# Column copies of a mixture-of-experts stage: a short loop of 32 copies with unchecked token numbers, the numbers brought in two transfers, and the first block's copies split over two engines

## What is computed

```
xs = ht[slot_tok].reshape(n_blocks, MOE_BLOCK, D)

def expert_block(args):
    xb, e = args
    return (jax.nn.silu(xb @ w_gate[e]) * (xb @ w_up[e])) @ w_down[e]

ys = lax.map(expert_block, (xs, blk_expert)).reshape(P, D)
ys = ys * slot_gate[:, None].astype(ys.dtype)
out = jax.ops.segment_sum(ys, slot_tok, num_segments=T)
```

## Time and profile before

| what | value |
|---|---|
| median of 3 runs | 1705.32 us (1703.37 to 1705.6) |
| the profiled execution, own time | 1699.97 us |
| its span, first to last instruction | 1698.2 us |
| mean granted TensorE clock | 0.976 of full speed |
| PE busy | 1550.6 us, 91% |
| DVE, POOL, ACT busy | 604.2, 451.5, 364.7 us |
| transfers over the span | 472.66 MB, mean 278 GB/s |
| GB/s in slices from about 720 us to the end | 366 to 428, but for the last (245) |

### The profile page before, as it was taken

The page is one execution under the profiler, slowest core; times in us unless marked ns, Lnnn a source line. Parts: engine busy times, 40 slices in busy tenths (PEclk is TensorE's granted clock), DMA queues, the critical chain, the costliest instruction groups (busy, mean ns, idle before and its releaser), DMA issues.

```text
span 1698.2 us, 25999 instructions
## 1 busy us (share of the span) xinstructions
PE 1550.6 (91%) x7036; PEld 857.2 (50%) x7036; DVE 604.2 (36%) x738; ACT 364.7 (21%) x695; POOL 451.5 (27%) x2197
## 2 busy tenths in 40 slices
PE   7999999999999999898988988888889988889897
PEld 7788777678886666533423323333323433333333
DVE  6655666542235334313303213212213312222224
ACT  6422333532222344211001001001001001001001
POOL 4560055310000000233233333223323333233220
PEclk9999999999999999999999999999999999999999
DMA  8333221542314025499999999999899999999996
GB/s 299 102 98 99 74 75 50 199 106 100 99 62 162 1 99 216 179 403 426 428 426 387 402 415 382 404 417 395 366 414 381 408 421 392 375 428 404 371 423 245
DMA packets 89099, 472.66 MB, mean 278 GB/s; under 512 B 5075, under 2 KB 43133, under 8 KB 62973
## 3 DMA queue, kind: packets, MB, share of 16 engines
q1 hardware_dynamic: 87944, 470.84, 69.1%
q0 software_dynamic: 912, 0.35, 0.4%
q10 hardware_dynamic: 100, 0.03, 0.0%
HBM read 466.99 MB, written 4.21 MB: 277 GB/s over the span
## 4 chain that ended last, share of the span: by engine, by line
PE 63%; DMA 26%; DVE 6%; ACT 2%; issue 2%; SPq 0%; DVEq 0%; POOL 0%; ACTq 0%
DMA weight_ring<-in_expert_w_up_dram 25%; PE ps L2283 19%; PE ps L1986 10%; PE ps L1860 10%; PE ps L2309 5%; PE ps L2242 4%; PE ps L2039 3%; DVE residual L1668 2%; PE ps L1822 1%; PE ps L2373 1%; DMA residual<-in_x_dram 1%; PE ps L2102 1%; ACT weight_ring L903 1%; PE ps L1915 1%; PE ps L2099 1%
## 5 line engine op out<-in xcount | busy, mean ns | idle before, releaser
L2283 PE MATMUL ps<-weight_ring,proj_buffer 128*64 128x512 f32 x2024 | 493.1, 619 | 69.3 <-DMA weight_ring<-in_expert_w_up_dram 63.6
L713 POOL COPY proj_buffer<-transposed_acts 128x16 f32 x1982 | 301.9, 212 | 559.8 <-issue 396.7
L2283 PEld LDWEIGHTS ps<-weight_ring,proj_buffer 128*64 128x64 f32 x2024 | 159.5, 142 | 388.7 <-issue 291.9
L1668 DVE TENSOR_TENSOR residual<-ps,residual 128x1024 f32<-128x1024 f32 x128 | 150.9, 1220 | 289.0 <-PE ps L2242 288.5
L2309 PE MATMUL ps<-weight_ring,proj_buffer 128*64 128x512 f32 x960 | 221.0, 614 | 19.5 <-DVE proj_buffer L1678 18.5
L1684 DVE SCALAR_TENSOR_TENSOR y_low<-ps,proj_buffer,y_high 64x1024 fp32r<-64x1024 f32 x60 | 77.0, 1283 | 243.6 <-ACT y_high L1096 242.7
L2309 PEld LDWEIGHTS ps<-weight_ring,proj_buffer 128*64 128x64 f32 x960 | 74.6, 141 | 148.4 <-issue 145.4
L1096 ACT ACTIVATE y_high<-ps,proj_buffer 64x1024 fp32r<-64x1024 f32 x60 | 66.6, 1109 | 296.7 <-PE ps L2309 295.9
L1085 ACT ACTIVATE proj_buffer<-ps 128x512 f32<-128x512 f32 x32 | 19.1, 598 | 485.7 <-PE ps L2283 485.7
L1860 PE MATMUL ps<-mix_high,w_in_high 128*128 128x512 f32 x288 | 117.3, 407 | 1.3 <-issue 1.3
L1860 PE MATMUL ps<-mix_high,w_in_low 128*128 128x512 f32 x288 | 112.3, 390 | 0.0
(11 more groups left out here) (326 smaller groups left out, 1830.4 us busy)
## 6 DMA issues: line engine op xcount, KB each, us to landing
weight_ring<-in_expert_w_down_dram SPq DMA_DIRECT2D x63, 2048.0 KB, 18.4
weight_ring<-in_expert_w_up_dram SPq DMA_DIRECT2D x61, 2048.0 KB, 22.9
weight_ring<-in_expert_w_gate_dram SPq DMA_DIRECT2D x61, 2048.0 KB, 17.8
weight_ring<-in_w_in_dram SPq DMA_DIRECT2D x18, 1024.0 KB, 5.5
weight_ring<-in_w_out_dram SPq DMA_DIRECT2D x16, 1024.0 KB, 5.0
weight_ring<-in_xkv_w_dram SPq DMA_DIRECT2D x8, 1024.0 KB, 7.4
residual<-in_x_dram SPq DMA_DIRECT2D x8, 1024.0 KB, 12.5
weight_ring<-in_expert_w_gate_dram SPq DMA_DIRECT2D x5, 1024.0 KB, 11.8
```

The source lines that it names most:

```text
L713: ins = g.tensor_copy(xsT[:, :, par * SLOTS + at + j], H[:, :, ds(where[j], 1)].rearrange("p k n -> p (k n)"))
L1668: v.tensor_tensor(part, ps[:, bank:bank + 2, :].rearrange("p b n -> p (b n)"), part, ALU.add).then_inc(signal, 1)
L2283: ins = mm(ps[side * SLOTS:(side + 1) * SLOTS, 0, :], xsT[:, k, par * SLOTS:(par + 1) * SLOTS], gate_up_weights(e, u, kk), start=(k == 0), ...
```

## The change

Six edits go together:

- **The short loop.** `copy_columns` makes one stretch of at most 32 columns. For blocks 2 to 31, POOL runs a loop over the blocks with a loop of two stretches inside. `block_rows` counts halves of a block, and PE waits for `b * 2 - 2`.
- **No checks.** The two checking instructions for each value are gone, on ACT too; the numbers are clamped where they are formed, before and after the change.
- **Token numbers.** They lie in DRAM as one row for each block. Blocks 2 to 5 come in one transfer of 1 KB, then all 32 blocks in one of 8 KB into a region of SBUF that is free once block 1's first unit is used. 16 transfers were made before, each issued inside the loop.
- **Block 0** is copied by ACT (36 columns, in two stretches of 18) and POOL (28). DVE's load, checks and 12 copies are gone. PE waits for two signals.
- **Block 1** is split in halves, 32 by ACT and 32 by POOL, and POOL does its half ahead of storing the token numbers to DRAM, which it did after block 0 before.
- The path for further blocks, which isn't taken here, is rewritten in the same way.

```diff
-BY_ACT, BY_DVE = 26, 12
+BY_ACT = 36
@@
-            def copy_columns(tokens, par, first, done, free=None, loaded=None):
-
-                for at in range(first, SLOTS, 32):
-                    n = min(32, SLOTS - at)
-                    _, where = nc.values_load_multi_w_load_instructions(
-                        tokens[:, at:at + n], engines=(mybir.EngineType.Pool,), min_val=0, max_val=S - 1)
-                    if at == 0 and free is not None:
-                        pool.wait_ge(gu_copied, free)
-                    if at + n == SLOTS and loaded is not None:
-                        loaded()
-                    for j in range(n):
-                        ins = g.tensor_copy(xsT[:, :, par * SLOTS + at + j], H[:, :, ds(where[j], 1)].rearrange("p k n -> p (k n)"))
-                ins.then_inc(done, 1)
+            def copy_columns(tokens, slots, before=None):
+
+                n = tokens.shape[1]
+                _, where = nc.values_load_multi_w_load_instructions(
+                    tokens, engines=(mybir.EngineType.Pool,), min_val=0, max_val=S - 1,
+                    skip_runtime_bounds_check_because=CLAMPED)
+                if before is not None:
+                    pool.wait_ge(gu_copied, before)
+                for j in range(n):
+                    ins = g.tensor_copy(slots[:, :, j], H[:, :, ds(where[j], 1)].rearrange("p k n -> p (k n)"))
+                return ins
@@
-            copy_columns(first_row[0:1, 0:SLOTS], 0, BY_ACT + BY_DVE, first_rows[0])
+            copy_columns(first_row[0:1, BY_ACT:SLOTS], xsT[:, :, BY_ACT:SLOTS]).then_inc(first_rows[0], 1)
+            copy_columns(first_row[0:1, SLOTS + 32:2 * SLOTS], xsT[:, :, SLOTS + 32:2 * SLOTS]).then_inc(first_rows[1], 1)
             pool.wait_ge(ids_ready, 1)
@@
-            load_ids(1)
-            with pool.Fori(1, NE // 2) as it:
-                pair_columns(it)
+            def block_columns(b, tokens, at):
+                before = pool.to_reg(b - 1)
+                first = pool.snap(b % 2 * SLOTS)
+                with pool.Fori(0, 2) as half:
+                    copy_columns(tokens[0:1, ds(at + half * 32, 32)],
+                                 xsT[:, :, ds(first + half * 32, 32)], before).then_inc(block_rows, 1)
+
+            load_ids(some_ids, 2, 4)
+            pool.wait_ge(block_ids_in, 16)
+            with pool.Fori(2, 6) as b:
+                block_columns(b, some_ids, b * SLOTS - 2 * SLOTS)
+            pool.wait_ge(used, UE + 7)
+            load_ids(all_ids, 0, NE)
+            pool.wait_ge(block_ids_in, 32)
+            with pool.Fori(6, NE) as b:
+                block_columns(b, all_ids, b * SLOTS)
@@
-            for par, n in enumerate((BY_ACT, 28)):
+            for par, first, last in ((0, 0, 18), (0, 18, BY_ACT), (1, 0, 32)):
@@
-            dve.wait_ge(h_turned, 56)
-            _, where = nc.values_load_multi_w_load_instructions(
-                first_row[0:1, BY_ACT:BY_ACT + BY_DVE], engines=(mybir.EngineType.DVE,), min_val=0, max_val=S - 1)
-            for j in range(BY_DVE):
-                ins = v.tensor_copy(xsT[:, :, BY_ACT + j], H[:, :, ds(where[j], 1)].rearrange("p k n -> p (k n)"))
-            ins.then_inc(first_rows[0], 1)
-
@@
-                    pe.wait_ge(first_rows[b], 3 - b)
+                    pe.wait_ge(first_rows[b], 2)
                 else:
-                    pe.wait_ge(block_rows, b - 1)
+                    pe.wait_ge(block_rows, b * 2 - 2)
```

More of the change, by code:

```diff
@@ L59 @@
 CUT = 3
-BY_ACT, BY_DVE = 26, 12
+BY_ACT = 36
+CLAMPED = "token numbers are sums of one-hot products over tokens, clamped to the last token where they are formed"
 def hybrid_block(nc, x, mem, mix_norm_g, w_in, q_norm_g, k_norm_g, sink_logits, pool_w, pool_scale,
@@ L66, in hybrid_block @@
                  expert_w_gate, expert_w_up, expert_w_down, out):
-    ids_dram = nc.dram_tensor("block_ids", (NBLK // 2 + 1, 2 * SLOTS), I32, kind="Internal").ap()
+    ids_dram = nc.dram_tensor("block_ids", (NBLK, SLOTS), I32, kind="Internal").ap()
     with ExitStack() as ctx:
@@ L161, in hybrid_block @@
         first_row = PB[0:1, 8768:8768 + 2 * SLOTS].bitcast(I32)
+        some_ids = PB[0:1, 8704:8704 + 4 * SLOTS].bitcast(I32)
+        all_ids = PB[0:1, 2048:2048 + NE * SLOTS].bitcast(I32)
         ids = PB[0:NBLK, 9112:9112 + SLOTS].bitcast(I32)
@@ L340, in hybrid_block @@
         ids_stored = sem("ids_stored")
-        pair_ids_in = sem("pair_ids_in")
+        block_ids_in = sem("block_ids_in")
         gu_copied = sem("gu_copied")
@@ L726, in _, with load_ids @@
             pool.wait_ge(ids_stored, 16)
[L728 to L736, removed]
-            load_ids(1)
-            with pool.Fori(1, NE // 2) as it:
-                pair_columns(it)
+            def load_ids(to, first, blocks):
+                pool.dma_start(to, ids_dram[ds(first, blocks), :].rearrange("b s -> (b s)").unsqueeze(0)).then_inc(block_ids_in, 16)
+            def block_columns(b, tokens, at):
[13 more added lines that the diff above has]
+                block_columns(b, all_ids, b * SLOTS)
             more = pool.value_load(meta[0:1, NOVER:NOVER + 1], min_val=0, max_val=NOVER)
             with pool.If(more > 0):
-                with pool.Fori(NE // 2, NBLK // 2) as it:
-                    pair_columns(it)
+                for first in range(NE, NBLK, 4):
+                    load_ids(some_ids, first, 4)
+                    pool.wait_ge(block_ids_in, 16 * (3 + (first - NE) // 4))
+                    with pool.Fori(first, first + 4) as b:
+                        block_columns(b, some_ids, b * SLOTS - first * SLOTS)
         @block.scalar
@@ L1105, in _ @@
             act.wait_ge(hT_ready, 56)
-            for par, n in enumerate((BY_ACT, 28)):
+            for par, first, last in ((0, 0, 18), (0, 18, BY_ACT), (1, 0, 32)):
                 _, where = nc.values_load_multi_w_load_instructions(
[L1108 to L1111, removed]
+                    first_row[0:1, par * SLOTS + first:par * SLOTS + last], engines=(mybir.EngineType.Activation,), min_val=0, max_val=S - 1,
+                    skip_runtime_bounds_check_because=CLAMPED)
+                for j in range(first, last):
+                    ins = a.activation(xsT[:, :, par * SLOTS + j], H[:, :, ds(where[j - first], 1)].rearrange("p k n -> p (k n)"), ACT.Copy)
+                if last >= 32:
+                    ins.then_inc(first_rows[par], 1)
             act.wait_ge(table_ready, 1)
```

3 lines of the change are left out of this document (1 added, 2 removed).

## The result

The changed kernel takes 1640.67 us (median of 4 runs, 1638.58 to 1642.86), the kernel before 1705.46 beside it (1703.37 to 1705.84). The ratio is 0.9623, with a 95% interval of 0.9606 to 0.964: 3.8% less time. The prediction said 1646.2, between 1636 and 1703.

A forecast was written before the change was run, and what follows sets the result against it. Transfers held back by one DMA engine, burdened with POOL's code, were taken to bound the kernel. Gains 56.7 + 2.4 = 59.1 us from 1699.97 gave 1640.9; plus 5.35 for the median, 1646.2, range 1636 to 1703.

The forecast's parts named there:

- The code step: POOL's short loop stays on the chip, its code packets go: 63.07 to 58.55 us a pair, 56.7 us in all.
- rival 1: In POOL's loop, code packets cost only their own time, 0.32 us each: 29 us gained, 1676; chance 0.14.
- Rival 2: The one slow DMA engine has nothing to do with code; only the first block counts: 1703; chance 0.08.
- half of a deficit of 14.3: Transfers' shortfall between 725 and 1676 us outside the eleven pairs; half counted as gain within the 56.7.
- The weak link: POOL's code fetched through one DMA engine, 0.72 us a packet; no row shows which engine carries the packets.
- POOL's work: Shorter POOL stretches in the loops, 13.25 to about 6.9 us, lie beside PE's work: counted as 0.
- its cover: POOL's work in the loops lies beside PE's 29 us a block; were this gone, at most 4.4 us.
- Token numbers: Two transfers in place of loads issued inside POOL's loop: 0, a few us once if block 2 were late.
- The first block: PE starts block 0 1.34 us earlier and its second half gains another 1.05: 2.4 us, bounds 1.3 and 2.8.
- The median: Whole execution: the median of runs stays 5.35 us above the profiled one, taking 1640.9 to 1646.2.
- Rival 3: POOL's short loop is fetched as well, so the kernel is slower; chance 0.16.

The follow-up runs named there:

- experiment 2: The changed kernel with POOL's second loop written out over four blocks in one body of 531 instructions: 1666.84 us.
- experiment 1: The changed kernel with the two checking instructions per token number put back in POOL's loops for blocks 2 to 31: 1655.9 us.
- experiment 4: The changed kernel with an added, unused 0.5 KB load of token numbers ahead of each block from 6 to 31, two a pair: 1641.03 us.
- experiment 8: The changed kernel with the first two blocks' copies as before (block 0 by ACT, DVE and POOL), all with checks: 1645.81 us.
- experiment 7: The changed kernel with POOL's second loop placed elsewhere in its code, at `head_slot` 220: 1641.83 us.
- experiment 3: The kernel before without the checks of the loop over pairs, its body 266 instructions instead of 522: 1641.95 us.
- experiment 9: The changed kernel run again, 1638.14 us; also with 8 constant matmuls ahead of block 0 in place of 20, 1638.71, and with none, 1637.03.
- experiment 6: The kernel before with checks in one stretch of four, 330 instructions, loop start set by `head_slot`: 1645.64 us at 0, 1696.55 at 100.

## Why the prediction was right

**The code step held, down to its size.** Of the eleven pairs I expected 49.7 us, 58.55 us a pair; they gave 47.6, 58.74 a pair, since the rate is 428 to 429 GB/s and not 430. The changed kernel, three others with packets and the one before lie nearly on one line:

| kernel | packets a pair | us a pair | us a packet above 58.74 |
|---|---|---|---|
| changed | 0 | 58.74 | |
| four blocks in a body | 2.8 | 60.77 | 0.73 |
| 394 instructions | 5.0 | 62.23 | 0.70 |
| 330, `head_slot` 100 | 5.1 | 62.55 | 0.75 |
| before | 6.27 | 63.07 | 0.69 |

That is the predicted 0.72, and rival 1 (0.32 each) is out: it gave 1652 for experiment 2, which took 1666.8. Rival 2 is out by the same table.

**Outside the eleven pairs the sum was right in part by luck.** There I had taken 7.0 us, half of a deficit of 14.3 with no row for the half, and 2.4 for the first block, 9.4 together. The profiles give 6.25 + 3.2 = 9.45. But that holds 2.72 us which the execution after had lost by the start of the 16 matmuls, and which no edit explains: from the 16 matmuls on, the gain outside the pairs is 12.2.

**The weak link stayed weak.** The window of share 0.06 and 25 GB/s has no more than the work of one engine of 16, and by the table a packet costs 0.69 to 0.75 us. What ties the two together is my argument. Such moments come with the packets: of the 720 windows of 1 us from 840 to 1560 the DMA share is under 0.10 in 14 before, in 12, 9 and 2 in the kernels of 330 (`head_slot` 100), 394 and 531 instructions, and in none of the ten profiles of kernels whose loop brings no packets. That the engine that is behind is the one that carries the packets is argued from this, not shown. Nor is it shown why a packet that fills an engine for 0.31 us costs over twice that.

**POOL's work: 0, but its cover was mis-sized.** A stretch went from 13.25 to 7.36 us and gave nothing by itself: experiment 2 has the same fast copies and loses 26 us of the gain. Yet with the checks in the short loop (experiment 1) a stretch has some 10.0 us of idle where 8.42 stood, and a block is 0.1 us over the transfers' 29.37, where I had counted with 27. I had named 4.4 us as the most that this could cost; it was 15. Two readings of mine were off. The checks of a stretch are some 7 us and not 8.42 - 2.07 = 6.35, for half of the register load lies under the copies ahead of it. And in the short loop the load comes behind those copies, 1.5 us later; so the changed kernel's stretch takes 7.36 and not 6.9.

**Token numbers: 0**, as predicted, and shown with twice the loads. That nothing else is on the queues, as I wrote against rival 1, was not quite so: 384 small packets of q0 stand in the window of the earlier trace rows. Experiment 4 shows that they cost nothing.

**The first block: right place, but its size hangs on the clock.** I gave 2.4 us, bounds 1.3 and 2.8. In the two profiles it is 25.83 - 22.91 = 2.9 up to the transposes, but then block 0's `down` takes 8.78 us where before had 7.09, and 1.2 are left at its end (35.17 us after the start of the 16 matmuls before, 33.94 after). By experiment 8 against 7 it is 4.0, by experiment 3 against 4, which ran beside each other, 0.9. PE began block 0 at 8.17 us after the start of the 16 matmuls, where I had 699.75 - 691.44 = 8.31. The part that I didn't have is the clock: old or new, the same 40 constants take 4.73 or about 6.4 us. The new order does not wait for columns in either case. The old one waits 1.34 us behind 6.43, and 3.8 behind 4.73, and then begins block 0 at a granted clock of 0.50 (experiment 8). The profiles of the kernels with no packets from 840 to 1560 and with `keep_busy(20)`, in us from the start of the 16 matmuls:

| first block | 40 constants take | transposes begin | block 6's second half of `gate_up` begins | whole execution |
|---|---|---|---|---|
| new, changed again (experiment 9) | 4.73 | 20.46 | 177.14 | 1638.14 |
| new, experiment 7 | 4.73 | 20.46 | 177.29 | 1640.48 |
| new, changed | 6.36 | 22.91 | 181.01 | 1642.86 |
| new, experiment 4 | 6.37 | 22.91 | 181.50 | 1643.06 |
| old, experiment 8 | 4.73 | 27.24 | 185.49 | 1646.85 |
| old, experiment 6 (`head_slot` 0) | 4.73 | 27.26 | 186.20 | 1645.27 |
| old, experiment 3 | 4.73 | 27.25 | 186.29 | 1646.0 |

So where the constants take 4.73 us the new order is 8 to 9 us ahead; the medians show less of it, as they would if they mix both cases. What the old order takes with 6.4 us is in no profile without packets. Experiment 3's other executions (1641.37 to 1642.09, against 1646.0 in the profile) may be that case.

**The median: a term of the sum that failed.** The sum for the profiled execution was 1640.9, and that took 1642.86. I then added 5.35, by which the three runs of before stood over their profile; after the change the median stood 2.2 below it. The prediction was 5.5 us high, and this term is 7.5 of it, less the 2.0 by which the sum was low. By the medians the gain is 1705.46 - 1640.67 = 64.8 us, where 59.1 was forecast. The profile of before was a short execution; its 16 matmuls began earlier than in any other profile here. Executions of the changed kernel fall into two groups, 1638.58 and 1639.21 against 1642.13 and 1642.86; experiment 4's do too (1638.78, 1639.01; 1643.06, 1643.19). The two clock cases of the first block differ by 2.45 us, and its first `down` by another 1.7 (7.09 and 8.78), 4.1 together, which fits. In the table above these 4 us are still there at block 6. Of the eight executions only 1642.86 and 1643.06 have a profile, both with the longer constants; for the others the clock case is argued.

**Rival 3 was wrong for this loop, and right in kind.** The short loop brings no packets, neither where it stands nor with `head_slot` 220 (experiment 7). But the place does decide for a longer one: the same 330 instructions bring none in ten pairs with `head_slot` 0, and 46 in nine pairs with 100. Bodies of 266 and less bring none, and 394, 522 and 531 bring 2.8 to 6.27 a pair. At about 130 instructions a packet, a body of 330 touches three or four packets' worth of code by where it begins, one of 266 mostly three and one of 394 four or more. My estimate is that POOL keeps a body over three of them and not one over four; it fits all of this, and the forecasts of experiment 6 came from such a reading. But where in the code a packet ends, and how many POOL keeps, stands in no trace. And all of it is POOL's: PE's loop is not short, as I had written, but carries out 232 matmuls and 232 weight loads in a pair of the changed kernel (933.91 to 992.65), and no queue there has a code packet between 840 and 1560 but q8, one.

## What to carry to other kernels

When transfers set the pace and yet fall short of their rate, look at the queues of instruction code (69 packets in eleven pairs here) and at windows of 2 us: a DMA share of 0.06, as from 1028 to 1030, is what one engine of 16 makes while the other 15 have nothing. A loop of an engine that nobody waits for cost some 4% here. On POOL it did so with 394 instructions and more, and with 330 at one of two places; with 266 it cost nothing. The cure is to leave out instructions or to start the loop at another place, not to speed up the engine. Take the offset between profile and median as a range, not as a term.

## What the runs showed of the hardware that I had not expected

- A kernel whose loop has the same 330 instructions took 1645.6 or 1696.6 us by the loop's place alone.
- 8 KB of code cost the 16 DMA engines' pace 0.69 to 0.75 us, as much as 0.3 MB of weights at 429 GB/s, and while 2.8 to 6.27 packets came in a pair the cost of each stayed the same.
- The clock of the same 40 constant matmuls ahead of block 0 differs between executions (4.73 or about 6.4 us). After a wait of 3.8 us (experiment 8) it stood at 0.50 from 706 to 710; after a wait of 1.34 the 34 matmuls of block 0 took 7.94.
- Without any matmul to keep TensorE busy ahead of block 0 the kernel was not slower: 1637.03 us, against 1638.14 beside it.
